# Deeper weight pieces for narrow regions, and five side stages reordered, in a four-layer kernel on one core

## The reference

```python
def layer_ab(x, ...):       # block 1, layer 1
    h = rms_norm(x, norm_g)
    g_q, g_k, g_v, g_lr, g_gate, f_q, f_k, f_v, f_f, f_gate = jnp.split(h @ w_in, split_idx, axis=-1)
    # gated linear attention (GLA, 4 heads) and forgetting attention (FOX, 8 heads)
    return x + jnp.concatenate([o_gla, o_fox], axis=-1) @ w_out

def layer_c(x, ...):        # block 1, layer 2: S5, 128 groups of 16 channels, 64 complex states
    u, gate = jnp.split(h @ w_in, 2, axis=-1)
    y = s5_ssm(u, ...)
    z = jax.nn.gelu(y); z = z * jax.nn.sigmoid(z @ glu_w + glu_b)
    return x + (z * jax.nn.silu(gate)) @ w_out

def even_layer(h, ...):     # block 2, layer 1
    lru_x, lru_gate, q, k, v, swa_gate = split_cols(h @ w_in, EVEN_SPLITS)
    y_a = rg_lru(causal_depthwise_conv(lru_x, conv_w, conv_b), ...) * jax.nn.silu(lru_gate)
    y_b = sliding_window_gqa_sinks(q, k, v, sinks) * jax.nn.silu(swa_gate)

def odd_layer(h, ...):      # block 2, layer 2: latent attention (MLA) and differential attention (DIFF)
    c_q, c_kv, k_rope, mla_gate, dq, dk, dv, diff_gate = split_cols(h @ w_in, ODD_SPLITS)
```

## Time and profile before

| | |
|---|---|
| median of 3 runs | 3574.49 us (3568.2 to 3575.54) |
| profiled execution, its own time | 3577.43 us |
| its span, first to last instruction | 3575.6 us |
| PE busy | 3448.2 us, 96% of the span |
| DVE, ACT, POOL busy | 46%, 36%, 15% |
| granted PE clock, mean | 0.978 |
| products (L597), in all | 12744 |

### The profile page before, as it was taken

The page is one execution under the profiler, slowest core; times in us unless marked ns, Lnnn a source line. Parts: engine busy times, 40 slices in busy tenths (PEclk is TensorE's granted clock), DMA queues, the critical chain, the costliest instruction groups (busy, mean ns, idle before and its releaser), DMA issues.

```text
span 3575.6 us, 42129 instructions
## 1 busy us (share of the span) xinstructions
PE 3448.2 (96%) x16557; PEld 2743.6 (77%) x16557; DVE 1634.1 (46%) x2716; ACT 1297.5 (36%) x2031; POOL 520.6 (15%) x757
## 2 busy tenths in 40 slices
PE   7899999999999999999999899999999999999996
PEld 6687887887887777888887686788878867766885
DVE  7884654334334444344344635543324243455432
ACT  4443433343233333433242436433223323355422
POOL 0001212332110000101320100121000101110211
PEclk9999999999999999999999979999999999999998
DMA  5775433546348776544335233453424633433631
GB/s 170 233 218 197 128 104 112 153 146 213 118 159 212 212 189 165 183 141 141 118 118 165 90 117 107 133 189 123 136 84 131 206 102 109 139 107 92 215 130 71
DMA packets 281637, 525.08 MB, mean 147 GB/s; under 512 B 64765, under 2 KB 102212, under 8 KB 276320
## 3 DMA queue, kind: packets, MB, share of 16 engines
q1 hardware_dynamic: 224992, 336.60, 31.8%
q0 software_dynamic: 54272, 182.52, 15.1%
q10 hardware_dynamic: 2176, 3.28, 0.3%
HBM read 408.32 MB, written 113.97 MB: 146 GB/s over the span
## 4 chain that ended last, share of the span: by engine, by line
PE 74%; DVE 3%; ACT 2%; DMA 2%; issue 1%; POOL 0%; ACTq 0%; DVEq 0%; POOLq 0%
PE pg L597 64%; PE pm L1279 3%; PE pm L1308 2%; PE pm L1295 1%; PE pm L2334 1%; PE pm L2337 1%; DMA mx_g<-zt 1%; ACT whi L380 0%; PE pm L2322 0%; DVE d_x L2421 0%; DVE xa L693 0%; DMA m_lam<-in_l_lambda_k 0%; DVE r_y L1654 0%; PE pm L2313 0%; ACT stage L475 0%
## 5 line engine op out<-in xcount | busy, mean ns | idle before, releaser
L386 DVE TENSOR_TENSOR wlo<-raw,whi 128x1024 fp32r<-128x1024 f32 (+4 forms) x553 | 668.5, 1214 | 1374.4 <-ACT whi L380 1373.2
L380 ACT ACTIVATE whi<-raw 128x1024 fp32r<-128x1024 f32 (+4 forms) x553 | 554.7, 1008 | 1183.8 <-PE pg L597 1174.4
L597 PE MATMUL pg<-a_hi,whi 128*128 128x512 f32 x1856 | 751.3, 405 | 10.8 <-DVE wlo L386 5.1
L597 PE MATMUL pg<-a_hi,wlo 128*128 128x512 f32 x1856 | 737.3, 397 | 0.0
L597 PE MATMUL pg<-a_lo,whi 128*128 128x512 f32 x1856 | 733.8, 395 | 0.0
L597 PE MATMUL pg<-b_hi,whi 128*128 128x512 f32 x1552 | 617.5, 398 | 7.3 <-DVE wlo L386 5.2
L597 PE MATMUL pg<-b_hi,wlo 128*128 128x512 f32 x1552 | 610.7, 393 | 0.0
L597 PE MATMUL pg<-b_lo,whi 128*128 128x512 f32 x1552 | 608.6, 392 | 0.0
L597 PEld LDWEIGHTS pg<-a_hi,whi 128*128 128x128 f32 x1856 | 352.2, 190 | 92.5 <-issue 11.4
L597 PEld LDWEIGHTS pg<-a_hi,wlo 128*128 128x128 f32 x1856 | 351.3, 189 | 80.6 <-issue 1.3
L597 PEld LDWEIGHTS pg<-a_lo,whi 128*128 128x128 f32 x1856 | 351.9, 190 | 78.5 <-issue 2.9
(11 more groups left out here) (425 smaller groups left out, 3838.0 us busy)
## 6 DMA issues: line engine op xcount, KB each, us to landing
raw<-in_l_w_in SPq DMA_DIRECT2D x160, 512.0 KB, 3.7
raw<-in_ab_w_in SPq DMA_DIRECT2D x112, 512.0 KB, 3.8
zt<-stage POOLq DMA_DIRECT2D x141, 256.0 KB, 3.4
raw<-in_c_w_in SPq DMA_DIRECT2D x64, 512.0 KB, 5.3
raw<-in_l_w_out SPq DMA_DIRECT2D x64, 512.0 KB, 3.8
raw<-in_ab_w_out SPq DMA_DIRECT2D x32, 512.0 KB, 3.8
raw<-in_glu_w SPq DMA_DIRECT2D x32, 512.0 KB, 4.2
raw<-in_c_w_out SPq DMA_DIRECT2D x32, 512.0 KB, 3.6
```

The costliest lines, as they stand in the source:

```text
L380: nc.scalar.activation(used(whi, n), used(raw, n), ACT.Copy).then_inc(hi_ready, 1)
L386: nc.vector.tensor_tensor(used(wlo, n), used(raw, n), used(whi, n).bitcast(F32), ALU.subtract).then_inc(lo_ready, 1)
L597: ins = nc.tensor.matmul(pg[m][:r.rows(m), :r.cols()], lhsT, rhs, start=(kt == 0 and n_pass == 0), stop=(kt == r.kts - 1 and n_pass == 2))
```

## The change

1. `Region.pk`: a narrow region of sixteen k-tiles gets deeper pieces, as many k-tiles as fill 128 x 1024. The 24 columns and the 64 of the rope key go from eight pieces to one, the 256 of the last latent queries from eight to four, and the band's k and v become one region of 256 columns in form T in four pieces.
2. v of the band therefore lies in zt with channels on partitions; it is loaded to w_vt, turned by four PE transposes and copied by DVE at the head of the band attention.
3. GLA: g_kd is turned at the third level of its own head.
4. S5: all sixteen state products of a slice, then all sixteen of the input.
5. Attention: values of job j-3 before the turning of job j-2; for DIFF at a tile's end a step lies between (36 steps become 44).
6. LRU: softplus in r_sp, outside the overlay, worked out before C_OUT; lead 3 pieces and not 2; r_x loads wait only for the store of their own bank and stand before those of the gate weights.
7. Rotation: loads and DVE work as six steps beside MLA_KV, keys first. MLA's rope queries get full 128 rows, even heads in m_qr, odd ones in m_qs, the other half of each set to zero, so that keys are used whole.

```diff
+        self.pk = min(kts, PK * BLK // width) if kts == KT else PK
+        self.pitch = PK * BLK // self.pk
-        self.pieces = kts // PK
+        self.pieces = kts // self.pk
...
-        ("B", T(w0, L0["q"], 1024, "copy", "wq") + T(w0, L0["k"], 128, "copy", "wkv") + N(w0, L0["v"], 128, "wv")),
+        ("B", T(w0, L0["q"], 1024, "copy", "wq") + T(w0, L0["k"], 256, "copy", "wkv")),
...
-            for k in range(PK):
-                kt = q * PK + k
+            for k in range(r.pk):
+                kt = q * r.pk + k
...
-        turn_kd(0)
         yield
         for h in range(GH):
             for lv in range(1, LEVELS + 1):
                 scores(h, lv - 1)
                 if lv == 1 and h + 1 < GH:
                     gate_logits(h + 1)
+                if lv == 3:
+                    turn_kd(h)
                 yield
...
+            if 3 <= j < a.jobs + 3:
+                pv(j - 3)
+            if between_tiles(a, j):
+                yield
             if 2 <= j <= a.jobs + 1:
                 turn(j - 2)
-            if 3 <= j < a.jobs + 3:
-                pv(j - 3)
             yield
...
         def load(n):
             s = n % 2
-            pool.wait_ge(ru_e, 2)
+            pool.wait_ge(ru_e, 3)
+            r = PHASES[LRU_IN][1][0]
+            pool.wait_ge(stored[n % MT], 16 * (r.stage0[n % MT] + n // MT + 1))
...
+    def swa_values_pe(pe, steps):
+
+        pe.wait_ge(shared_in, 128)
+        for b in range(NTOK):
+            ins = nc.tensor.transpose(pm[3][:, b * P:(b + 1) * P], V3["w_vt"][:, b * P:(b + 1) * P], ident[:, :])
+        ins.then_inc(xt_ready, 1)
+        for n, _ in enumerate(steps):
+            if n == 2:
+                pe.wait_ge(xt_ev, 4 * NTOK + 1)
+            yield
...
         wait_stored(act, MLA_Q)
-        act.wait_ge(w_used, pieces_before(DIFF_KV))
+        act.wait_ge(w_used, pieces_before(MLA_KV))
...
+        run(vec.tensor_tensor(q[even], q[even], qs[even], ALU.add))
+        run(vec.tensor_tensor(qs[odd], q[odd], qs[odd], ALU.add))
+        yield
+        run(vec.memset(q[odd], 0.0))
+        run(vec.memset(qs[even], 0.0))
...
-            (V4["m_qr"][half(t), t // 2, qb * P:(qb + 1) * P], V4["m_kr"][half(t), :count * P])],
+            (V4["m_qr" if t % 2 == 0 else "m_qs"][:, t // 2, qb * P:(qb + 1) * P], V4["m_kr"][:, :count * P])],
...
             for j in range(SPAIR):
                 for n in range(2):
                     nc.tensor.matmul(y_of(j), V6["d_x"][:, n, j, :, :].rearrange("p g k -> p (g k)"),
-                                     V6["d_C"][:, n, j, 1:, :], start=(n == 0), stop=False)
+                                     V6["d_C"][:, n, j, 1:, :], start=(n == 0 and j % 4 == 0), stop=False)
+            for j in range(SPAIR):
                 for g in range(2):
                     ins = nc.tensor.matmul(y_of(j)[g * SK:(g + 1) * SK, :], V6["d_UT"][:, 2 * j + g, :], V6["d_MG"][:, 2 * (2 * (j % 4) + g) + j // 4, :],
-                                           start=False, stop=True)
+                                           start=False, stop=(j % 4 == 3))
...
-        beside(lru_pe(pe), LRU_STEPS, pe, pe_piece, SWA_IN, 2)
-        rest = beside(after(shared_in, 128, pe, att_pe(pe, SWA)), SWA.steps, pe, pe_piece, L0_GATES, 4, TAIL)
+        beside(lru_pe(pe), LRU_STEPS, pe, pe_piece, SWA_IN, 3)
+        rest = beside(swa_values_pe(pe, att_pe(pe, SWA)), SWA.steps, pe, pe_piece, L0_GATES, 4, TAIL)
...
-        beside(after_rope(after(rope_done, 1, pe, att_pe(pe, MLA))), ROPE_STEPS + MLA.steps, pe, pe_piece, DIFF_KV, 4)
+        beside(after(rope_done, 1, pe, att_pe(pe, MLA)), MLA.steps, pe, pe_piece, DIFF_KV, 4)
...
+        softplus_act(act)
         in_turn(products(act, C_OUT, act_piece))
         in_turn(products(act, LRU_IN, act_piece))
-        beside(lru_act(act), LRU_STEPS, act, act_piece, SWA_IN, 2)
+        beside(lru_act(act), LRU_STEPS, act, act_piece, SWA_IN, 3)
...
-        in_turn(products(act, MLA_KV, act_piece))
-        beside(after_rope(att_act(act, MLA), lambda: rope_loads(act), lambda: rope_act(act)), ROPE_STEPS + MLA.steps, act, act_piece,
-               DIFF_KV, 4)
+        beside(rope_act(act), ROPE_STEPS, act, act_piece, MLA_KV, 2)
+        beside(att_act(act, MLA), MLA.steps, act, act_piece, DIFF_KV, 4)
```

More of the change, by code:

```diff
@@ L90, in __init__ @@
         self.units = self.jobs * comps
-        self.steps = self.jobs + 4
+        self.steps = self.jobs + 4 + (tiles if gain is not None else 0)
 def count_regions(regions):
@@ L221, in serial, with window @@
         return run
[L224 to L225 removed]
+    def window(w, width=BLK):
+        pk = min(KT, PK * BLK // width)
+        return lambda i, q, c0: w[q * pk * P:(q + 1) * pk * P, bass.ds(c0 + i * BLK, BLK)].rearrange(
             "(k p) n -> p k n", p=P)
@@ L240, in T @@
             lo = n // BLK * BLK
-            made.append(Region(window(w), KT, c0 + lo, 1, n % BLK, "T", evac, to_zt(dst, at + lo)))
+            made.append(Region(window(w, n % BLK), KT, c0 + lo, 1, n % BLK, "T", evac, to_zt(dst, at + lo)))
         return made
     def beside_in_one(w, parts, evac, dst):
-        r = Region(window(w), KT, parts[0][0], 1, sum(n for _, n in parts), "T", evac, to_zt(dst))
+        width = sum(n for _, n in parts)
+        r = Region(window(w, width), KT, parts[0][0], 1, width, "T", evac, to_zt(dst))
         r.joined, at = [], 0
@@ L365, in sp_piece @@
             load_piece(sp, r.piece0 + i * r.pieces + q + LOAD_AHEAD)
-    used_columns = [r.width for _, rs in PHASES for r in rs for _ in range(r.blocks * r.pieces)]
+    used_columns = [(r.width, r.pk) for _, rs in PHASES for r in rs for _ in range(r.blocks * r.pieces)]
     def used(ring, n):
-        w = used_columns[n]
-        return ring[:, n % RING, :] if w == BLK else ring[:, n % RING, :].rearrange("p (k c) -> p k c", k=PK)[:, :, :w]
+        w, pk = used_columns[n]
+        whole = ring[:, n % RING, :]
+        return whole if w * pk == PK * BLK else whole.rearrange("p (k c) -> p k c", k=pk)[:, :, :w]
     def split_hi(act, n):
@@ L1267, in place, with between_tiles @@
         return j // a.per, j // NTOK % a.heads, BLOCK_ORDER[j % NTOK]
+    def between_tiles(a, j):
+        return a.gain is not None and j >= a.per + 3 and (j - 3) % a.per == 0
     def att_pe(pe, a):
@@ L1315, in square_sum @@
             nc.tensor.matmul(pm[2][:, :], ones[:, :], a.buf["sq"][:, :], start=True, stop=True).then_inc(att["ss"], 1)
-        for j in range(a.steps):
-            if a.gain is not None and j >= a.per + 3 and (j - 3) % a.per == 0:
+        for j in range(a.jobs + 4):
+            if between_tiles(a, j):
                 square_sum((j - 3) // a.per - 1)
@@ L2534, in after @@
             yield
-    ROPE_STEPS = 5
-    def after_rope(steps, first=None, last=None):
-        for n in range(ROPE_STEPS):
-            if n == 0 and first is not None:
-                first()
-            if n == ROPE_STEPS - 1 and last is not None:
-                last()
-            yield
-        for step in steps:
-            yield
     TAIL = 6
@@ L2608, in _ @@
         in_turn(products(pool, LRU_IN, pool_piece))
-        beside(lru_pool(pool), LRU_STEPS, pool, pool_piece, SWA_IN, 2)
+        beside(lru_pool(pool), LRU_STEPS, pool, pool_piece, SWA_IN, 3)
         rest = beside(att_pool(pool, SWA), SWA.steps, pool, pool_piece, L0_GATES, 4, TAIL)
@@ L2616, in _ @@
         in_turn(products(pool, MLA_KV, pool_piece))
-        beside(att_pool(pool, MLA, ROPE_STEPS), ROPE_STEPS + MLA.steps, pool, pool_piece, DIFF_KV, 4)
+        beside(att_pool(pool, MLA), MLA.steps, pool, pool_piece, DIFF_KV, 4)
         rest = beside(att_pool(pool, DIFF), DIFF.steps, pool, pool_piece, L1_GATES, 4, TAIL)
@@ L2693, in _ @@
         mixed(z_dve(dve), rest, dve, dve_piece, C_GLU)
+        softplus_dve(dve)
         in_turn(products(dve, C_OUT, dve_piece))
         in_turn(products(dve, LRU_IN, dve_piece))
-        beside(lru_dve(dve), LRU_STEPS, dve, dve_piece, SWA_IN, 2)
-        rest = beside(att_dve(dve, SWA), SWA.steps, dve, dve_piece, L0_GATES, 4, TAIL)
+        beside(lru_dve(dve), LRU_STEPS, dve, dve_piece, SWA_IN, 3)
+        rest = beside(swa_values_dve(dve, att_dve(dve, SWA)), SWA.steps, dve, dve_piece, L0_GATES, 4, TAIL)
         mixed(mix_dve(dve, 1, A["a_lo"]), rest, dve, dve_piece, L0_OUT)
@@ L2701, in _ @@
         in_turn(products(dve, MLA_Q, dve_piece))
-        in_turn(products(dve, MLA_KV, dve_piece))
-        beside(after_rope(att_dve(dve, MLA), None, lambda: rope_dve(dve)), ROPE_STEPS + MLA.steps, dve, dve_piece, DIFF_KV, 4)
+        beside(rope_dve(dve), ROPE_STEPS, dve, dve_piece, MLA_KV, 2)
+        beside(att_dve(dve, MLA), MLA.steps, dve, dve_piece, DIFF_KV, 4)
         rest = beside(att_dve(dve, DIFF), DIFF.steps, dve, dve_piece, L1_GATES, 4, TAIL)
```

129 lines of the change are left out of this document (76 added, 53 removed).

## The result

The changed kernel takes **3453.3 us** (median of 4 runs, 3450.5 to 3455.3) against 3575.0 of the kernel before: a ratio of 0.966 with an interval of 0.965 to 0.967, 122 us less. Forecast were 3461 and a range of 3438 to 3498. The profiled execution took 3455.26 us, its span 3453.5, its mean clock 0.988 after 0.978.

The account below looks back on a forecast made before the run. TensorE was taken to bound the kernel: its products at 0.230 us each, its waits and the lower clock after them. Terms summed to -113.2 us, from the 3575.0 median to 3461, range 3438 to 3498.

Parts of the forecast that it names:

- Deep piece in GLA_IN: Low-rank and forget columns in GLA_IN: one piece of sixteen k-tiles for eight removes idle and low clock; -17 us (-8 to -22).
- GLA's keys: FOX_IN: turning decayed keys two steps later removes the g_kd waits, last head's gain taken over by output-tile wait; -6.6 us.
- S5's order: S5 slices: sixteen state then sixteen input products save 2.3 us in each of eight slices; -18.5 us (0 to -21).
- Softplus: Recurrence's softplus placed before C_OUT: small operations and a table load delay C_OUT's wlo; +3 us (0 to +4).
- SWA_IN and the band: Recurrence beside SWA_IN's projections, v in turned form: 148 us against 180.5, with a new 4 us wait; -32.5 (-24 to -40).
- Latent regions: Latent and k-rope pieces: the wait for stage stays, two are a little shorter; -0.5 us (-4 to 0).
- Rotation: Rotation beside MLA_KV: 12.1 us lost before, 2.6 left for ACT's splits and evacuations queuing behind load issue; -9.5 us.
- MLA's rows: MLA jobs: full rows for rope keys save 0.34 us per job over 32 jobs; -10.6 us (-12 to 0).
- DIFF: DIFF attention: values before turning and a step between cut m_rs waits (13.8 us) and clock loss (10.6); -21 us (-24 to -12).
- waits only move, DVE late again: Rival: DVE late again, so GLA_IN gives 5 us, SWA_IN 20, DIFF 12; 3495 us in all; 15%.
- The rule by columns: Rival: cost follows columns, not rows, so v's form (30 us) and MLA's rows (10.6) give nothing; 3502 us; 4%.
- The clock did not stay low over wide products: Denies a rival: SWA_IN's low clock persists through k and v, 96 wide products taking 41 us, not 22; 3480 us; 8%.

Follow-up runs that it names:

- after64: Changed kernel with 64 more unused bytes per partition ahead of the overlays, so activations lie at an odd multiple of 64 bytes again: 3476.7 us, ratio 0.973.
- s5_alone: Kernel before with only S5's order changed (sixteen state products, then sixteen input products): 3554.3 us, ratio 0.994.

## Why the prediction was right, and where it was not

The time lay in the range, 8 us below the forecast, but that it came so near is luck: two errors met. Without the price of products the edits gave some 94 to 98 us where I had 113.2, and a cause that I had not seen gave 23 to 28. With the old price it would have been 3476.7 (after64), still in the range, but 16 us above the forecast.

- **Deep piece in GLA_IN:** -17 forecast; -13.5 by the phase and 13.5 by undoing it. The mechanism was right, down to the clock. By the row below PE's idle time in the phase fell from the 19.4 us of the earlier trace rows to 10.0, by 9.4 where I had 10; eight small waits for s_L remain, 5.7 us in all, none above 1.0. The clock stood low for 12.7 us of the phase and not for 27.7, worth at most 7.5 where I had 7, and less as far as the low clock fell into waits. What of the missing 3.5 is due to that I did not separate.

```profile
29.00:304.70 275.70, 265.67 (x1425) 0.98 0.71 216
```

- **GLA's keys:** -6.6; -2.9 by the phase and 0.4 to 2.1 by undoing. The step that failed is that only the last head's gain would be taken over. The first head's was too, by g_qe (2.1 us), which DVE makes after g_kd; the last head's wait for g_o grew from 1.3 to 3.9, as forecast.
- **S5's order:** -18.5; -19.4 alone. Right, and so was the mechanism; 5.6 us for a slice had been 5.7.
- **Softplus:** +3; +2.3. Right.
- **SWA_IN and the band:** -32.5; -29.8, of which v's form alone is 29.2 less the transposes. The wait for stage at the first block's end was forecast at 4 us and is 3.2; the first pair's was forecast to stay, and stayed, though its releaser is r_ga and no longer r_x.
- **Latent regions:** -0.5; -2.9. The stage wait was halved (2.1 to 0.9), and the low clock behind it went too, but that is hardly the change's doing: s5_alone, with the old pieces, waits for 2.6 us there, keeps the clock at full and has a DIFF_Q of 96.5 us against 98.2 before and 96.0 after.
- **Rotation:** -9.5; +5.7 in MLA_KV, and DIFF_KV less 23.6, of which the rows are 12.3: -5.6. ACT issued the loads from 2708.44 to 2719.63 us, 11.2 us where the old place took 8.7, and its splits and evacuations piled up behind, as the timeline of ACT in the changed kernel shows. I had left 2.6 for that; it was 5.7 in this trace, and 2.0 to 6.8 in the traces of the five other kernels with the same code there (MLA_KV 46.0 to 50.8 us), so the size is not sharp.

```profile
2708.44 2.41 ACTq L1873 DMA_DIRECT2D m_cs<-in_rope  x1
...
2719.74 2.00 ACT L386 ACTIVATE whi<-raw 128x1024 fp32r<-128x1024 f32 x2 [10.86 <-PE pg L603]
2721.65 2.04 ACT L494 ACTIVATE stage<-pg 128x512 f32<-128x512 f32 x4
```

- **MLA's rows:** -10.6; 12.3 by undoing. Right.
- **DIFF:** -21; -10.4 by the phase, 6.6 by undoing. This is the term that was wrong by most. I had taken the whole of the clock's loss (10.6) as the waits' due and costed the new order at nothing. But the clock's share changes from kernel to kernel under the same waits: low for 20.5 us in this phase before and for 10.2 in s5_alone, whose waits are the same 15.0 us. And the order costs 3.1 us. Of my signs of being right, "no wait for m_rs above 1 us" failed: one of 2.1 is left.
- **Not in the sum at all:** 228.9 ns a product was read correctly and taken as a constant. It was 2.2 ns above what the same product costs from a better place, and in form N nearly 6. (A slip beside it: 480 x 0.230 is 110.4, not 110.2, which moves nothing.)

The rivals: the first (waits only move, DVE late again) did not come. GLA_IN gave 13.5 and not 5, SWA_IN 29.8 and not 20. DIFF gave no more than its 12, but by another way: the wait for m_rs went nearly whole, and clock and order took the rest. Only the decayed keys in FOX_IN, which it did not name, behaved so. The rule by columns is out by 29.2 and 12.3 us. The clock did not stay low over wide products.

## What to carry to other kernels

Look at the phases that a change does not touch before you credit those that it does; a uniform difference is neither schedule nor work, and here a tensor added ahead of the large buffers was a fifth to a quarter of the gain. Where one instruction is nearly the whole time, try the distance of its two operands in memory as one tries a tile size. A wait taken away at the queue that is late can come back at the next thing that this queue makes (4.8 of 7.0 us in FOX_IN); a form taken away (narrow products, a change between heights or row counts on PE) stayed away in every one of these kernels. Before you credit an edit with the low clock behind a wait, look at another kernel with the same wait.

## What I had not expected of the hardware

- The pace of TensorE's products depends on where the stationary and the moving operand lie to one another: 226.7, 228.9 and 233.3 ns for distances of 0, 64 and 128 bytes by 256 with the weights stationary, and in C_U0, with the activation stationary, 227.4, 233.2 and 232.4. Both activation buffers start at the same remainder in all kernels. Distances that are no multiple of 64 were not tried, and why the distance matters no run tells.
- Narrow products hold the clock low without a wait. In two kernels PE was busy for 41.0 us at 0.50, 36 of them over 192 products of 128 columns; that they bring it down by themselves is likely, not shown.
- A change of form on PE costs about 0.35 us there and back between full-height and half-height outputs, and about 0.2 us for each change between operands of 128 and 64 rows (12.3 us for 64 of them). That the cost lies in the change and not in the smaller product is shown for the first by two run lengths; for the second by the full-row product behind, which is 0.11 us longer.
